# Rotary products on the tensor engine replaced by copies between partitions, in the sparse mixer of a two-block decoder

## The chip, the cores and the metric

One core of one Trainium2 chip. The metric is the device time of one execution in microseconds (us), the median of several runs. The kernel before takes 2184.75 us (median of 3 runs, 2183.49 to 2184.96). All data are float32; the matrix products of the weights are made in three passes on values split into a high and a low part.

## The reference, cut to what matters

The program is two decoder blocks of two mixers each on 512 tokens of width 1024. The change lies in the last mixer, the sparse attention ("NSA"), between its input projection and its scores:

```python
def rope(x, positions):                       # dh = 64
    inv = ROPE_THETA ** (-jnp.arange(0, dh, 2) / dh)
    ang = positions[..., None] * inv
    x1, x2 = jnp.split(x, 2, axis=-1)
    return jnp.concatenate([x1 * cos - x2 * sin, x2 * cos + x1 * sin], axis=-1)

p = h @ w_in                                  # 512 x 3632
q, kc, vc, ks, vs, kw, vw, gl, z = jnp.split(p, splits, axis=-1)
q = rope(q.reshape(B, S, 16, 64)) * 64 ** -0.5
kc, ks, kw = rope(...), rope(...), rope(...)  # 4 groups of 64 each
kcmp = compress(kc, pe_k, ck_w1, ck_w2)       # windows of 32 keys, stride 16, a small MLP
vcmp = compress(vc, pe_v, cv_w1, cv_w2)
# three softmax attentions of q: over kcmp/vcmp, over ks/vs, over kw/vw; gated and summed,
# times silu(z), and the product with w_out
```

## The kernel before, in words

Every engine has one program in a fixed order, written out by hand; engines meet through semaphores. The tensor engine runs the products; the scalar engine (ACT) makes the high part of each weight part ("WH", line 508), the vector engine (DVE) the low part ("WL", `dve_weights`, line 511), from "RAW", which the SP queue loads 1 MB (two parts) at a time into two buffers (`sync_weights`, line 495). WH and WL have three buffers, so the high part of part j waits until part j-3 has been used.

A feature (`feat`, line 585) is 24 products of 128x128 by 128x512 (8 pieces of the contraction, three passes each) into one PSUM bank: 128 rows of the projection (two heads or two groups of 64), 512 tokens wide. In the sparse mixer the tensor engine's program `pe_nsa` (line 2412) makes the gate logits and q features 0 and 1 together, turns the gate logits, makes q features 2 to 7, then the pairs kc0, kc1, vc0, vc1, ks0, ks1, the token products of the values (line 2460), `compress(0)`, kw0, kw1, more token products, `compress(1)`, and then the scores. "kc0" is the feature with groups 0 and 1 of the compressed keys.

The rotation (rope) swaps the two halves of each head, with a sign, and mixes them with cosines and sines. Before, the tensor engine makes the swap as a product with a permutation matrix that holds the sign:

- `rotate_q(m)` in `pe_nsa` (line 2421): one product of 128x128 by 128x512 on the copy of feature m that ACT has put into the temporary TM (line 2589). It stands one feature late: after feature m+1.
- `rotate_k(kind, pair)` (line 2426): for each of the two groups of the pair, one product that spreads the group over both halves of the partitions ("rda"), and one that spreads its swapped form ("rdb"); so four products for kc, ks and kw, and two for vc, which isn't rotated.
- DVE's `rotate_q` (line 2705) multiplies the product with the sines, TM with the cosines, and adds: three operations of 128x512. DVE's `rotate_k` (line 2713) does the same on each group, six operations a pair (eight for kc, whose second half is stored one token late, in "X2").
- ACT's `rotate_k` (line 2592) copies the spread vc from PSUM to X2.
- DVE's `gather` (line 2735) reads X2 for `compress`; the scores read KS and KW.

TM has four buffers in a ring. `turns()` (line 287) lists who takes them in turn and what must be done before the buffer is free: entry i waits for the end of entry i-4. Before, a q feature takes one entry, and the buffer of feature m is used again by feature m+4.

GpSimd (POOL) loads the mixer's constants and small weights, among them the first-layer weights of `compress(0)` (2 MB, "w1"), then waits for the end of `compress(0)` to load those of `compress(1)` into the same place (line 2912), and works again only in the scores (`share`).

Of the kernel before, what the change touches and what calls it, by code (L numbers as in the profile page):

```python
# [25 lines left out]
L_M, L_R, L_N = 0, 128, 640  # L26
N_NM, N_P, N_DA, N_DB, N_N = 0, 512, 640, 896, 1152
N_CM, N_CN, N_BD, N_IR, N_INV, N_N2 = 0, 128, 256, 260, 264, 266


def constants():
# [27 lines left out]

    def rot(src):  # L60

        m = np.zeros((128, 128), np.float32)
        for d in range(128):
            base, e = src[d]
            if e < 32:
                m[base + e + 32, d] = -1
            else:
                m[base + e - 32, d] = 1
        return m

    n[:, N_P:N_P + 128] = rot([(64 * (d // 64), d % 64) for d in range(128)])
    for par in range(2):
        a = np.zeros((128, 128), np.float32)
        for d in range(128):
            a[64 * par + d % 64, d] = 1
        n[:, N_DA + 128 * par:N_DA + 128 * par + 128] = a
        n[:, N_DB + 128 * par:N_DB + 128 * par + 128] = rot([(64 * par, d % 64) for d in range(128)])
    for t in range(4):
# [7 lines left out]
    inv = np.float32(10000.0) ** (-np.arange(0, 64, 2, dtype=np.float32) / np.float32(64))  # L86
    n2[:, N_INV] = inv.astype(np.float32)[p % 32]
    return {"c_base": c, "c_gdn": g, "c_alibi": b, "c_gla": l, "c_nsa": n, "c_nsb": n2}
# [98 lines left out]
class Book:  # L187
# [25 lines left out]
    def at(self, *event):  # L213
        if not self.known:
            return None, 0
        name, n = self.value[event]
        return self.sem(name), n
# [69 lines left out]
def turns():  # L287

    out = []
# [47 lines left out]
    out.append((("few", "n"), ("full", "few_t", "n")))  # L337
    out.extend((("rq", m), ("q", m)) for m in range(8))

    def rotated(kind, pair):  # L340
        if kind != "vc":
            for g in (2 * pair, 2 * pair + 1):
                out.extend((("rj", kind, g, i), ("kv", kind, g)) for i in range(2))

    before = None
    for kind, pair in (("kc", 0), ("kc", 1), ("vc", 0), ("vc", 1), ("ks", 0), ("ks", 1), ("kw", 0), ("kw", 1)):
        if before:
            rotated(*before)
        out.append((("rk", kind, pair), ("full", "rda" if kind == "vc" else "rdb", kind, pair, 1)))
        before = kind, pair  # L350
    rotated(*before)
    out.extend((("r4", g), ("full", "vcb")) for g in range(4))
# [5 lines left out]
def bass_decoder_pair(nc, I, K, out):  # L358
    with ExitStack() as ctx:
# [1980 lines left out]
        NM = CS[:, N_NM:N_NM + 512]  # L2340
        PRM = CS[:, N_P:N_P + 128]
        PE_R = slot(11)[0:32, 0:128]
# [41 lines left out]
        def value_gather(x, g):  # L2384

            x.wait_ge(*ps.free("rda", "vc", g // 2, g % 2))

# [24 lines left out]
        def pe_nsa(p):  # L2412
# [7 lines left out]

            def rotate_q(m):
                p.wait_ge(*ps.free("nq", m))
                p.wait_ge(*at("c_nsa"))
                several(p, ("nr", m), lambda b: [(b[:, :], PRM, tm("rq", m))])

            def rotate_k(kind, pair):
                p.wait_ge(*ps.free("nk", kind, pair))
                for par in range(2):
                    for name, col0 in (("rda", N_DA), ("rdb", N_DB)):
                        if name == "rda" or kind != "vc":  # L2430
                            several(p, (name, kind, pair, par), lambda b: [
                                (b[:, :], CS[:, col0 + 128 * par:col0 + 128 * par + 128], tm("rk", kind, pair))])

            def compress(i):
# [9 lines left out]
            for m in range(8):  # L2444
                if m >= 2:
                    feat(p, ("nq", m), NSA)
                if m:
                    rotate_q(m - 1)
            before = None
            for i, kind in enumerate(n_steps):  # L2450
                if kind:
                    feat(p, ("nk", *kind), NSA)
                if before:
                    rotate_k(*before)
                elif i == 0:
                    rotate_q(7)
                before = kind
                if not kind:
                    br = i // 7
                    toks(p, ("nvv", br), normed(NSA), 2, "V")  # L2460
                    if br:
                        p.wait_ge(*ps.free("cmp", 0, 1))
                        p.wait_ge(*at("w2_twice"))
                        job = ("keys",)
                        b = ps.take(*job)
                        p.wait_ge(*ps.empty(*job))
                        chain(p, PS[b][:, 0:128], [(W2D[:, m, :, :].rearrange("p e d -> p (e d)"), HD[:, 0, m, :])
                                                   for m in range(2)]).then_inc(*ps.filled(*job))
                    compress(br)
# [11 lines left out]
            def scores(u):  # L2481
# [8 lines left out]
                if br is None:  # L2490
# [8 lines left out]
                    return  # L2499
                p.wait_ge(*at("kv", "kw" if br else "ks", 3))  # L2500
                p.wait_ge(*at("mask"))
# [80 lines left out]
        def act_nsa(a):  # L2582
# [8 lines left out]

            def rotate_k(kind, pair):
                if kind == "vc":
                    for par in range(2):
                        g = 2 * pair + par
                        ba = bank("rda", kind, pair, par)
                        a.wait_ge(*ps.full("rda", kind, pair, par))
                        a.do.copy(X2[1][0:64, g, :], ba[0:64, :])
                        a.do.copy(X2[1][64:128, g, 0:511], ba[64:128, 1:512]).then_inc(*ps.read("rda", kind, pair, par))

            def compress(i):
                for m in range(2):
                    a.wait_ge(*ps.full("cmp", i, m))
                    act(a, HD[:, i, m, :], bank("cmp", i, m)[:, 0:128], ACT.Silu).then_inc(*ps.read("cmp", i, m))

            before = None
            for i, kind in enumerate(n_steps):
                if before:
                    rotate_k(*before)
                if kind:  # L2610
# [4 lines left out]
                else:  # L2615
# [7 lines left out]
                    compress(br)  # L2623
                before = kind

# [66 lines left out]
        def dve_nsa(v):  # L2692
# [12 lines left out]
            def rotate_q(m):  # L2705
                x, q = tm("rq", m), NQ[:, m, :]
                v.wait_ge(*ps.full("nr", m))
                v.wait_ge(*at("sines"))
                tt(v, q, bank("nr", m)[:, :], SIN, ALU.mult).then_inc(*ps.read("nr", m))
                step(v, tt(v, x, x, COS, ALU.mult))  # L2710
                tt(v, q, q, x, ALU.add).then_inc(*up("q", "q", m))

            def rotate_k(kind, pair):
                for par in range(2):
                    if kind == "vc":
                        continue
                    g = 2 * pair + par
                    job = (kind, pair, par)
                    t1, t2 = tm("rj", kind, g, 0), tm("rj", kind, g, 1)
                    v.wait_ge(*ps.full("rda", *job))  # L2720
                    v.wait_ge(*tm_clear("rj", kind, g, 0))
                    tt(v, t1, bank("rda", *job)[:, :], COS, ALU.mult).then_inc(*ps.read("rda", *job))
                    v.wait_ge(*ps.full("rdb", *job))
                    v.wait_ge(*tm_clear("rj", kind, g, 1))
                    tt(v, t2, bank("rdb", *job)[:, :], SIN, ALU.mult).then_inc(*ps.read("rdb", *job))
                    v.wait_ge(*ps.free("rda", *job))
                    v.wait_ge(*ps.free("rdb", *job))
                    if kind == "kc":
                        tt(v, X2[0][0:64, g, :], t1[0:64, :], t2[0:64, :], ALU.add)
                        m = tt(v, X2[0][64:128, g, 0:511], t1[64:128, 1:512], t2[64:128, 1:512], ALU.add)  # L2730
                    else:
                        m = tt(v, (KS if kind == "ks" else KW)[:, g, :], t1, t2, ALU.add)
                    m.then_inc(*up("kv", "kv", kind, g))

            def gather(i, piece):
# [6 lines left out]
                for g in (0, 1) if piece == 1 else (2, 3):  # L2742
                    if i:
                        value_gather(v, g)
                    else:
                        v.wait_ge(*at("kv", "kc", g))
                    base = X2[i][:, g, :]
# [145 lines left out]
        def pool_nsa(g):  # L2893
# [17 lines left out]
            load(g, "w1", ("w1", 0), W1, I["nsa_ck_w1_2"][0].rearrange("(l p) n -> p l n", p=128))  # L2911
            g.wait_ge(*ps.full("cmp", 0, 1))
            load(g, "w1", ("w1", 1), W1, I["nsa_cv_w1_2"][0].rearrange("(l p) n -> p l n", p=128))
            for i in range(-1, NT):
# [158 lines left out]
```

## Time and profile before

| | |
|---|---|
| median of 3 runs | 2184.75 us |
| the profiled execution's own time | 2184.13 us |
| its span in the profile | 2182.3 us |
| tensor engine (PE) busy | 2044.2 us, 94% of the span |
| VectorE (DVE) busy | 1081.5 us, 50% |
| ScalarE (ACT) busy | 901.0 us, 41% |
| GpSimd (POOL) busy | 178.3 us, 8% |
| mean granted clock of the tensor engine | 0.976 of full speed |

Times in the rows are microseconds from the span's start. The sparse mixer's projection runs from about 1735 to 1912, its scores and output product from there to the end. A row of the timeline tells start, length, engine, line, operation, what it writes and reads, and in brackets how long its engine had been idle and who released it. Matrix products overlap: the distance between two starts, not the length, tells what one costs. A float32 product of this kind leaves two records.

### The profile page before, as it was taken

To read this page: it belongs to the slowest core of one execution; us is meant where nothing else is said; L and a number is where in the kernel's file an instruction comes from. 1 tells how busy PE (TensorE), PEld (TensorE's weight loads), DVE (VectorE), ACT (ScalarE), POOL (GpSimd) and SP (SyncE) were. 2 spreads that over 40 slices of the span, in tenths; PEclk is the share of its full clock that TensorE was granted. 3 is DMA by queue.
4 is the path that set the end of the run, shared out by engine and by line. 5 is a ranking of instruction groups with operands and counts; after the bars stand their busy time and mean duration, and the time that the engine had idled before them with its cause. 6 is when DMAs were issued, how large, how long until landed. Compare 5 with 4: busy or idle time off the path is not lost. (4 is left out here: it accounts for less than half of the span.)

```text
span 2182.3 us, 27453 instructions
## 1 busy us (share of the span) xinstructions
PE 2044.2 (94%) x11261; PEld 1630.5 (75%) x11261; DVE 1081.5 (50%) x1728; ACT 901.0 (41%) x1661; POOL 178.3 (8%) x138
## 2 busy tenths in 40 slices
PE   7969989999999989999999999989999799989988
PEld 5758868888887777657888888767887677856567
DVE  4556545434435442674544343545255545455763
ACT  5552234323324553674432231464343522245562
POOL 1011000000000000440000000000000100033440
PEclk9989999999999999999999999998999899999999
DMA  4211112332322223111323332213321322210001
GB/s 140 74 58 40 40 58 87 97 97 97 97 97 78 77 86 97 39 39 58 107 97 96 97 97 97 78 53 98 97 68 39 96 95 75 80 39 20 20 2 68
DMA packets 117682, 162.41 MB, mean 74 GB/s; under 512 B 6074, under 2 KB 80070, under 8 KB 117558
## 3 DMA queue, kind: packets, MB, share of 16 engines
q1 hardware_dynamic: 114502, 150.47, 21.3%
q0 software_dynamic: 2768, 9.14, 1.4%
q8 instruction: 90, 1.47, 0.3%
q10 hardware_dynamic: 288, 1.05, 0.1%
q14 instruction: 34, 0.28, 0.0%
HBM read 158.55 MB, written 2.10 MB: 74 GB/s over the span
## 5 line engine op out<-in xcount | busy, mean ns | idle before, releaser
L438 DVE TENSOR_TENSOR WL<-RAW,WH 128x1024 fp32r<-128x1024 f32 (+1 forms) x283 | 346.0, 1225 | 410.4 <-ACT WH L508 409.9
L508 ACT CAST WH<-RAW 128x1024 fp32r<-128x1024 f32 (+1 forms) x283 | 292.8, 1037 | 401.1 <-PE PSUM L542 399.6
L542 PE MATMUL PSUM<-XH,WH 128*128 128x512 f32 (+4 forms) x1128 | 428.2, 380 | 7.0 <-DVE XL L438 3.6
L542 PE MATMUL PSUM<-XH,WL 128*128 128x512 f32 (+4 forms) x1128 | 415.2, 368 | 0.0
L542 PE MATMUL PSUM<-XL,WH 128*128 128x512 f32 (+4 forms) x1128 | 415.1, 368 | 0.0
L542 PE MATMUL PSUM<-WH,HP 128*128 128x512 f32 x1024 | 318.0, 390 | 1.9 <-DVE WL L438 1.9
L542 PE MATMUL PSUM<-WH,XH 128*128 128x512 f32 (+1 forms) x608 | 242.2, 398 | 20.2 <-DVE WL L438 13.4
L542 PEld LDWEIGHTS PSUM<-XH,WH 128*128 128x128 f32 (+3 forms) x1128 | 213.7, 189 | 48.6 <-issue 7.4
L542 PEld LDWEIGHTS PSUM<-XL,WH 128*128 128x128 f32 (+3 forms) x1128 | 213.2, 189 | 40.1 <-issue 6.3
L542 PEld LDWEIGHTS PSUM<-XH,WL 128*128 128x128 f32 (+3 forms) x1128 | 212.8, 189 | 35.5
L542 PE MATMUL PSUM<-WL,XH 128*128 128x512 f32 (+1 forms) x608 | 233.7, 384 | 0.0
L542 PE MATMUL PSUM<-WH,XL 128*128 128x512 f32 (+1 forms) x608 | 233.5, 384 | 0.0
L542 PEld LDWEIGHTS PSUM<-WH,HP 128*128 128x128 f32 x1024 | 192.3, 188 | 42.4 <-DVE WL L438 2.8
L455 ACT ACTIVATE TM<-PSUM 128x512 f32<-128x512 f32 x128 | 75.9, 597 | 317.8 <-PE PSUM L542 291.3
L542 PE MATMUL PSUM<-WL,HP 128*128 128x512 f32 x512 | 199.2, 389 | 0.0
L542 PEld LDWEIGHTS PSUM<-WH,XH 128*128 128x128 f32 x608 | 116.7, 192 | 49.7 <-DVE WL L438 16.6
L542 PEld LDWEIGHTS PSUM<-WL,XH 128*128 128x128 f32 x608 | 116.9, 192 | 22.9 <-issue 2.6
L542 PEld LDWEIGHTS PSUM<-WH,XL 128*128 128x128 f32 x608 | 116.5, 192 | 22.6
L438 DVE TENSOR_TENSOR TM<-TM 128x512 f32<-128x512 f32 x64 | 44.3, 692 | 173.9 <-ACT TM L455 173.4
L542 PEld LDWEIGHTS PSUM<-WL,HP 128*128 128x128 f32 x512 | 96.1, 188 | 19.9
L550 PE MATMUL PSUM<-AR 64*64 64x64 f32 (+6 forms) x1424 | 99.4, 262 | 10.2 <-ACT TM L455 6.7
L550 PEld LDWEIGHTS PSUM<-AR 64*64 64x64 f32 (+3 forms) x1424 | 75.9, 151 | 32.0 <-issue 20.0
(237 smaller groups left out, 2526.2 us busy)
## 6 DMA issues: line engine op xcount, KB each, us to landing
RAW<-in_w_mlp_dram SPq DMA_DIRECT2D x64, 1024.0 KB, 5.3
RAW<-in_nsa_w_in_dram SPq DMA_DIRECT2D x14, 1024.0 KB, 5.0
RAW<-in_w_in_e_dram SPq DMA_DIRECT2D x12, 1024.0 KB, 5.2
RAW<-in_w_qkv_o_dram SPq DMA_DIRECT2D x12, 1024.0 KB, 5.1
RAW<-in_gla_w_in_dram SPq DMA_DIRECT2D x12, 1024.0 KB, 5.2
RAW<-in_w_ple_gate_dram SPq DMA_DIRECT2D x8, 1024.0 KB, 5.0
RAW<-in_w_out_e_dram SPq DMA_DIRECT2D x4, 1024.0 KB, 4.9
RAW<-in_w_out_o_dram SPq DMA_DIRECT2D x4, 1024.0 KB, 5.1
```

The source lines that it names most:

```text
L438: return x.do.tensor_tensor(o, a, b, op)
L455: return a.do.activation(o, i, func, **kw)
L508: a.do.copy(hi, r).then_inc(*up("w_hi", "w_hi", j))
L542: m = p.do.matmul(o, l, r, start=start and i == 0, stop=stop and i == len(pairs) - 1)
L550: m = p.do.matmul(o, l, r, start=True, stop=True)
```

## The change

For q, kc, ks and kw the halves of each head are swapped by four DMAs of 32 partitions each, from one TM buffer ("rq" or "rk") to another ("rb"), issued by POOL (`swap_halves`). The sign stands in the frequencies of the constant, so the sines have it. DVE then rotates a whole pair of groups at once, in TM, with three operations of 128x512. For the keys four more DMAs of 64 partitions each spread the two groups over both halves of the partitions, straight into KS, KW or X2 (`spread`), one token late for the second half of X2. The permutation products, their constants (640 of the 1152 columns of c_nsa) and ACT's copies of vc are gone. The swap of q feature m takes two entries of the ring of TM. The first-layer weights of `compress(1)` are loaded from ACT's queue, since POOL is busy with other things there.

```diff
-    n[:, N_P:N_P + 128] = rot([(64 * (d // 64), d % 64) for d in range(128)])
...
-    n2[:, N_INV] = inv.astype(np.float32)[p % 32]
+    n2[:, N_INV] = np.where(p % 64 < 32, -1, 1) * inv.astype(np.float32)[p % 32]
...
-    out.extend((("rq", m), ("q", m)) for m in range(8))
...
+    for m in range(8):
+        out.extend(((("rq", m), ("q", m)), (("rb", m), ("q", m))))
+    for kind, pair in (("kc", 0), ("kc", 1), ("vc", 0), ("vc", 1), ("ks", 0), ("ks", 1), ("kw", 0), ("kw", 1)):
+        out.append((("rk", kind, pair), ("moved", kind, pair)))
         if kind != "vc":
+            out.append((("rb", kind, pair), ("rope", kind, pair)))
...
         def value_gather(x, g):
-            x.wait_ge(*ps.free("rda", "vc", g // 2, g % 2))
+            x.wait_ge(*at("moved", "vc", g // 2))
...
             for m in range(8):
                 if m >= 2:
                     feat(p, ("nq", m), NSA)
-                if m:
-                    rotate_q(m - 1)
-            before = None
             for i, kind in enumerate(n_steps):
                 if kind:
                     feat(p, ("nk", *kind), NSA)
-                if before:
-                    rotate_k(*before)
-                elif i == 0:
-                    rotate_q(7)
...
-                p.wait_ge(*at("kv", "kw" if br else "ks", 3))
+                for pair in range(2):
+                    p.wait_ge(*at("moved", "kw" if br else "ks", pair))
...
             def compress(i):          # ACT
...
+                if i == 0:
+                    load(a, "w1_values", ("w1", 1), W1, I["nsa_cv_w1_2"][0].rearrange("(l p) n -> p l n", p=128))
...
             def rotate_q(m):          # DVE
-                x, q = tm("rq", m), NQ[:, m, :]
-                v.wait_ge(*ps.full("nr", m))
+                x, y, q = tm("rq", m), tm("rb", m), NQ[:, m, :]
+                v.wait_ge(*at("rb", m))
                 v.wait_ge(*at("sines"))
-                tt(v, q, bank("nr", m)[:, :], SIN, ALU.mult).then_inc(*ps.read("nr", m))
+                tt(v, q, y, SIN, ALU.mult)
                 step(v, tt(v, x, x, COS, ALU.mult))
                 tt(v, q, q, x, ALU.add).then_inc(*up("q", "q", m))
 
             def rotate_k(kind, pair):
...
+                if kind == "vc":
+                    return
+                x, y = tm("rk", kind, pair), tm("rb", kind, pair)
+                v.wait_ge(*at("rb", kind, pair))
+                tt(v, y, y, SIN, ALU.mult)
+                step(v, tt(v, x, x, COS, ALU.mult))
+                tt(v, x, x, y, ALU.add).then_inc(*up("rope", "rope", kind, pair))
...
-            g.wait_ge(*ps.full("cmp", 0, 1))
-            load(g, "w1", ("w1", 1), W1, I["nsa_cv_w1_2"][0].rearrange("(l p) n -> p l n", p=128))
+            def swap_halves(*job):
+                x, y = tm("rq" if len(job) == 1 else "rk", *job), tm("rb", *job)
+                g.wait_ge(*ps.free(*(("nq",) if len(job) == 1 else ("nk",)), *job))
+                g.wait_ge(*tm_clear("rb", *job))
+                sem = f"swapped{tm_at['rb', *job] % 4}"
+                for d in range(4):
+                    s = d + 1 - 2 * (d % 2)
+                    load(g, sem, ("rb", *job) if d == 3 else (), y[32 * d:32 * d + 32, :], x[32 * s:32 * s + 32, :])
+
+            def spread(kind, pair):
+                x = tm("rk", kind, pair)
+                g.wait_ge(*(ps.free("nk", kind, pair) if kind == "vc" else at("rope", kind, pair)))
+                sem = f"spread{tm_at['rk', kind, pair] % 4}"
+                for par in range(2):
+                    src = x[64 * par:64 * par + 64, :]
+                    for r in range(2):
+                        last = ("moved", kind, pair) if par and r else ()
+                        if kind in ("ks", "kw"):
+                            load(g, sem, last, (KS if kind == "ks" else KW)[64 * r:64 * r + 64, 2 * pair + par, :], src)
+                        else:
+                            load(g, sem, last, X2[kind == "vc"][64 * r:64 * r + 64, 2 * pair + par, 0:512 - r], src[:, r:512])
+
+            for m in range(8):
+                swap_halves(m)
+            before = None
+            for kind in n_steps:
+                if kind and kind[0] != "vc":
+                    swap_halves(*kind)
+                if before:
+                    spread(*before)
+                before = kind
```

## Rows read from the trace of the kernel before

**Rows 1.** The page's first part: engines' busy time, share, instructions.

```profile
PE 2044.2 (94%) x11261; PEld 1630.5 (75%) x11261; DVE 1081.5 (50%) x1728; ACT 901.0 (41%) x1661; POOL 178.3 (8%) x138
```

**Rows 2.** Busy time in stretches of the mixer: PE, PEld, DVE, ACT, POOL, clock, DMA share.

```profile
1784.00:1803.00 19.00, 19.00 (x79) 14.63 (x78) 9.35 (x12) 4.60 (x6) 0.00 (x0) 1.00 0.22 70
1803.00:1835.00 32.00, 32.00 (x121) 22.41 (x120) 20.21 (x27) 10.78 (x16) 0.00 (x0) 1.00 0.17 58
```

**Rows 3.** Groups of PE instructions by shape, 1747 to 1912.

```profile
L550 PE MATMUL PSUM<-TM,CS 128*128 128x512 f32 x72 | 33.8, 596 | 4.1 <-ACT TM L455 3.0 <-ACT TM L2613 1.1
```

**Rows 4.** Timeline of PE: permutation products of q and of keys, and a feature.

```profile
1783.97 1.02 PE L550 MATMUL PSUM<-TM,CS 128*128 128x512 f32 x2
...
1787.37 0.39 PE L542 MATMUL PSUM<-XH,WL 128*128 128x512 f32 x1
...
1790.09 0.39 PE L542 MATMUL PSUM<-XH,WL 128*128 128x512 f32 x1
1790.32 1.02 PE L550 MATMUL PSUM<-TM,CS 128*128 128x512 f32 x2
...
1803.01 3.59 PE L550 MATMUL PSUM<-TM,CS 128*128 128x512 f32 x8
...
1820.79 1.88 PE L550 MATMUL PSUM<-TM,CS 128*128 128x512 f32 x4
...
1827.99 1.88 PE L550 MATMUL PSUM<-TM,CS 128*128 128x512 f32 x4
```

**Rows 5.** Timeline of PE where q feature 0 is swapped, and the next product.

```profile
1747.25 0.24 PE L557 MATMUL PSUM<-CB,AR 32*128 32x32 f32 x1
1750.54 1.13 PE L550 MATMUL PSUM<-TM,CS 128*128 128x512 f32 x2 [3.04 <-ACT TM L455]
...
1758.59 1.02 PE L550 MATMUL PSUM<-TM,CS 128*128 128x512 f32 x2
```

**Rows 6.** Busy time and granted clock just behind that wait.

```profile
1751.10:1755.10 4.00, 4.00 (x11) 2.99 (x10) 1.98 (x3) 0.00 (x0) 0.00 (x0) 0.58 0.18 60
```

**Rows 7.** Timeline of PE: the products of ks1 and kw1.

```profile
1839.33 3.70 PE L550 MATMUL PSUM<-TM,CS 128*128 128x512 f32 x8 [0.53 <-ACT TM L2613]
...
1876.58 3.70 PE L550 MATMUL PSUM<-TM,CS 128*128 128x512 f32 x8 [0.54 <-ACT TM L2613]
```

**Rows 8.** Timeline of ACT: the copies of q features 0 and 1, and a later step.

```profile
1749.91 1.07 ACT L455 ACTIVATE TM<-PSUM 128x512 f32<-128x512 f32 x2
...
1790.52 0.60 ACT L455 ACTIVATE TM<-PSUM 128x512 f32<-128x512 f32 x1 [4.81 <-PE PSUM L542]
```

**Rows 9.** Timeline of DVE: the rotation of one q feature and a low part.

```profile
1785.03 0.69 DVE L438 TENSOR_TENSOR AR<-PSUM,AR 128x512 f32<-128x512 f32 x1 [3.20 <-PE PSUM L550]
...
1786.96 1.22 DVE L438 TENSOR_TENSOR WL<-RAW,WH 128x1024 fp32r<-128x1024 f32 x1
```

**Rows 10.** Timeline of POOL: an issue and its next work; DVE beside the issue.

```profile
1734.02 1.22 DVE L438 TENSOR_TENSOR WL<-RAW,WH 128x1024 fp32r<-128x1024 f32 x1
...
1734.94 0.50 POOL L463 DMA_DIRECT2D AR<-in_nsa_pe_k_dram  x1
...
1861.99 1.15 POOL L463 DMA_DIRECT2D AR<-in_nsa_cv_w_dram  x1 [122.89 <-PE PSUM L542]
1920.63 0.61 POOL L438 TENSOR_TENSOR AR<-AR,ST 128x256 f32<-128x256 f32 x1 [57.49 <-DVE ST L438]
```

**Rows 11.** DMA issues by tensor: KB each, us from issue to landing.

```profile
AR<-in_gla_w_gk_up_dram POOLq DMA_DIRECT2D x1, 32.0 KB, 3.3
out_dram<-H SPq DMA_DIRECT2D x4, 512.0 KB, 2.6
AR<-in_nsa_pe_v_dram POOLq DMA_DIRECT2D x1, 8.0 KB, 4.8
AR<-in_nsa_b_gate_dram POOLq DMA_DIRECT2D x1, 24.0 KB, 7.7
AR<-in_nsa_cv_w_dram POOLq DMA_DIRECT2D x1, 2048.0 KB, 10.2
```

More of the change, by code:

```diff
@@ L26 @@
 L_M, L_R, L_N = 0, 128, 640
-N_NM, N_P, N_DA, N_DB, N_N = 0, 512, 640, 896, 1152
+N_NM, N_N = 0, 512
 N_CM, N_CN, N_BD, N_IR, N_INV, N_N2 = 0, 128, 256, 260, 264, 266
@@ L58, in constants @@
     n[:, N_NM:N_NM + 512] = np.where(x <= j, 0, NEG)
[L60 to L69, printed above, removed]
-    n[:, N_P:N_P + 128] = rot([(64 * (d // 64), d % 64) for d in range(128)])
[L72 to L77, printed above, removed]
     for t in range(4):
@@ L337, in turns @@
     out.append((("few", "n"), ("full", "few_t", "n")))
-    out.extend((("rq", m), ("q", m)) for m in range(8))
-    def rotated(kind, pair):
+    for m in range(8):
+        out.extend(((("rq", m), ("q", m)), (("rb", m), ("q", m))))
+    for kind, pair in (("kc", 0), ("kc", 1), ("vc", 0), ("vc", 1), ("ks", 0), ("ks", 1), ("kw", 0), ("kw", 1)):
+        out.append((("rk", kind, pair), ("moved", kind, pair)))
         if kind != "vc":
-            for g in (2 * pair, 2 * pair + 1):
-                out.extend((("rj", kind, g, i), ("kv", kind, g)) for i in range(2))
-    before = None
-    for kind, pair in (("kc", 0), ("kc", 1), ("vc", 0), ("vc", 1), ("ks", 0), ("ks", 1), ("kw", 0), ("kw", 1)):
-        if before:
[L348 to L351, printed above, removed]
+            out.append((("rb", kind, pair), ("rope", kind, pair)))
     out.extend((("r4", g), ("full", "vcb")) for g in range(4))
@@ L2340, in bass_decoder_pair @@
         NM = CS[:, N_NM:N_NM + 512]
-        PRM = CS[:, N_P:N_P + 128]
         PE_R = slot(11)[0:32, 0:128]
@@ L2419, in pe_nsa @@
             turned(p, ("pec",), lambda b: [(b[:, 0:32], PE_R)])
[L2421 to L2432, printed above, removed]
             def compress(i):
@@ L2446, in pe_nsa @@
                     feat(p, ("nq", m), NSA)
-                if m:
-                    rotate_q(m - 1)
-            before = None
             for i, kind in enumerate(n_steps):
@@ L2452, in pe_nsa @@
                     feat(p, ("nk", *kind), NSA)
-                if before:
-                    rotate_k(*before)
-                elif i == 0:
-                    rotate_q(7)
-                before = kind
-                if not kind:
+                else:
                     br = i // 7
@@ L2590, in act_nsa @@
                 act_weights(a, first_part["nq", m] + 3)
[L2592 to L2599, printed above, removed]
             def compress(i):
@@ L2604, in compress @@
                     act(a, HD[:, i, m, :], bank("cmp", i, m)[:, 0:128], ACT.Silu).then_inc(*ps.read("cmp", i, m))
-            before = None
+                if i == 0:
+                    load(a, "w1_values", ("w1", 1), W1, I["nsa_cv_w1_2"][0].rearrange("(l p) n -> p l n", p=128))
             for i, kind in enumerate(n_steps):
-                if before:
-                    rotate_k(*before)
                 if kind:
@@ L2623, in act_nsa @@
                     compress(br)
-                before = kind
             def z_gate(m):
@@ L2713, in rotate_k @@
             def rotate_k(kind, pair):
[L2714 to L2733, printed above, removed]
+                if kind == "vc":
[5 more added lines that the diff above has]
+                tt(v, x, x, y, ALU.add).then_inc(*up("rope", "rope", kind, pair))
             def gather(i, piece):
@@ L2745, in gather @@
                     else:
-                        v.wait_ge(*at("kv", "kc", g))
+                        v.wait_ge(*at("moved", "kc", g // 2))
                     base = X2[i][:, g, :]
@@ L2911, in pool_nsa @@
             load(g, "w1", ("w1", 0), W1, I["nsa_ck_w1_2"][0].rearrange("(l p) n -> p l n", p=128))
-            g.wait_ge(*ps.full("cmp", 0, 1))
-            load(g, "w1", ("w1", 1), W1, I["nsa_cv_w1_2"][0].rearrange("(l p) n -> p l n", p=128))
+            def swap_halves(*job):
[16 more added lines that the diff above has]
+                            load(g, sem, last, (KS if kind == "ks" else KW)[64 * r:64 * r + 64, 2 * pair + par, :], src)
+                        else:
+                            load(g, sem, last, X2[kind == "vc"][64 * r:64 * r + 64, 2 * pair + par, 0:512 - r], src[:, r:512])
[8 more added lines that the diff above has]
+                before = kind
             for i in range(-1, NT):
```

## The prediction, made before the change was timed

> **What bounds the kernel now.** I read the page first [rows 1]: the tensor engine is busy for 94% of the span, the vector engine for 50%, POOL for 8%. An average says nothing of one stage, so the table by stretches comes next [rows 2]: from 1784 to 1835 PE is busy for all of the time, DVE for 9.35 of 19.00 us and 20.21 of 32.00 us, at a full clock, while the DMA engines are busy for 0.22 and 0.17. In this stage a microsecond taken off PE should be a microsecond of the kernel, as long as nothing new is late. What the change takes off PE is one group [rows 3]: 72 records, 36 products (8 for q, 24 for kc, ks, kw, 4 for vc), 33.8 us busy and 4.1 us of idle time ahead of them, which waited for ACT's copies.
>
> **What goes from PE.** Busy times overlap, so I price a product by starts [rows 4].
> - A feature: from 1787.37 to 1790.09 there are 12 starts, 0.2267 us each; 24 make 5.44 us.
> - A q step is 1790.32 - 1783.97 = 6.35, so a q product costs 6.35 - 5.44 = 0.91; eight: 7.3 us.
> - A rotated pair: from kc0's products to vc0's, two steps, 1820.79 - 1803.01 = 17.78, so 8.89 a step; less 5.44 is 3.45; six pairs: 20.7 us.
> - vc: 1827.99 - 1820.79 = 7.20, less 5.44 is 1.76; two: 3.5 us. Together 31.5 us.
> - The wait of q product 0 for ACT's copy, 3.04 us [rows 5]. After the change nothing on PE waits for that copy; the next feature's parts are made by then.
> - The clock behind that wait. From product 0 to product 1 it is 1758.59 - 1750.54 = 8.05 us against 6.35 in the later step: 1.70 us. The row of that stretch shows a granted clock of 0.58, near the lower level of 1.2 GHz, where the later stretches have 1.00 (2.4 GHz) [rows 6, 2]. PE had been idle just before. Without the idle time I expect no fall: 1.7 us more.
> - The waits ahead of the products of ks1 and kw1, 0.53 + 0.54 = 1.1 us [rows 7].
> Sum: 31.5 + 3.0 + 1.7 + 1.1 = 37.3 us.
>
> **What comes in its place, q.** Say feature m ends at t. ACT's copy starts about 0.2 later and takes 0.5 to the next start (two take 1.07 [rows 8]). POOL issues four DMAs; an issue takes 0.50 [rows 10], so the fourth starts 1.5 after the first. No row shows a copy from SBUF to SBUF. Bounds for the landing from its issue: 2.6 us for a store of 512 KB (SBUF is its source), 7.7 us for 24 KB that queued behind other loads; the nearest row by size and queue is 32 KB on POOL's queue, 3.3 us [rows 11]. I take 3.3. Then DVE needs three operations, from 1785.03 to 1786.96, 1.93 us [rows 9], the same number as before. End: t + 0.2 + 0.5 + 0.1 + 1.5 + 3.3 + 1.9 = t + 7.5. Two deadlines follow.
> - The ring of TM. The copy of feature m+2 now needs q(m), since a feature takes two entries; it comes up at t + 10.9. Slack 3.4 us.
> - DVE's order. Behind the blocked rotation of m stands the low part that is used four features on, which starts at t + 16.3; it is done at t + 7.5 + 1.2 [rows 9]. Slack over 7 us in the steady run, but less at the start, as copies 0 and 1 are late (1749.91 and about 1750.4 [rows 8]): swap 0 can't start before 1750.6, q(0) is done at 1757.2, then copy 2, its high part, the rotation of 1 and the low part of feature 5 at 1760.4. PE, running from 1747.4 at 5.44 a step, wants that part at 1763.8: slack 3.4 us, the tightest place.
>
> **The keys.** Let kc0 end at T. POOL has kc1's swap ahead of kc0's spread, so: swap of kc1 from T + 6.3 to T + 8.3, four issues of the spread to T + 10.3, the last one's landing 3.3 after its start at T + 9.8: T + 13.1. ACT's copy of vc0 waits for that buffer, 2 us beyond vc0's end, and with it the high part behind it on ACT (T + 14.6) and the low part on DVE (T + 15.8). ks1 uses it at T + 21.8: slack 6 us. I carried all programs through such a schedule, step by step, to the scores: with 3.3 us PE never waits. It stays so up to a landing of 4.5 us; 5.0 costs 0.4, 6.7 costs 8.5 and 7.7 costs 14.5 us. Run on the program before, the same schedule gives its end within 1 us, once the 1.7 of the clock are added.
>
> **Edits at no cost, with their cover.** DVE's six or eight operations a pair become three: less on an engine that waits [rows 2]. ACT's eight copies of vc go. The smaller constant lands sooner; nobody waits for it. POOL's 88 new issues, 44 us at 0.50 [rows 10], lie in its empty stretch: one issue stands between about 1739 and 1920. Loading w1 for compress(1) from ACT: issued at the end of compress(0), as before, it lands 10.2 us later [rows 11]; two features (10.9) and the value products stand between: over 10 us of slack. ACT's issue delays kw0's copy, which has that feature's 5.4 us as cover. If this cover goes, compress(1) waits. The scores' new wait for ks stands 45 us behind the spread. The transfers, 3.6 MB of swaps and 4 MB of spreads, meet SP's loads, 1 MB every two steps; the DMA share is about 0.2 there [rows 2]. A swap that meets such a load may take 5 to 6 us; in the schedule that is every other one, and those may be 6 us late in landing before PE stands.
>
> **A rule weighed against a row.** An issue at 1734.94 takes 0.50 us although DVE is at a subtraction with two operands from SBUF until 1735.24 [rows 10]. The Trainium skill (SBUF — State Buffer, "The 'DVE blocks DMA' trap (SWDGE)") says that a DVE operation in a two-port mode, as a float32 copy has, locks POOL out, so that it cannot write descriptors. DVE has no such copy beside the swaps, only two memsets; with each issue at the 0.50 of the row the sum stands, and with the issues of one swap held back by up to the 3.4 us of slack above it would stand too.
>
> **The numbers.** The profiled execution has 2184.13 us, its span 2182.3, and the median is 2184.75, 0.6 above. 2184.13 - 37.3 = 2146.8; on the median 2147.5. That is the forecast, and alone it would lie between 2146 and 2149.
>
> **Rivals.**
> - **Late landings, some given back.** The four transfers of a swap meet SP's loads or each other, and the last lands after 6 to 9 us. For: 7.7 us for only 24 KB in a full queue [rows 11]. Against: there the queue had 1 MB loads and more ahead of it. The schedule gives back 5 to 24 us: 2152 to 2171, about 2159 at 7 to 7.5 us. Chance 0.18.
> - **The transfers run one after another (slower).** If POOL's transfers don't overlap but each pays its whole latency, the queue, not PE, sets the pace. From q 0 to ks1 there are 72 (48 of swaps, 24 of spreads) against about 72 us of features: PE waits from 1.3 us each, and from 1.75 us each all 37 us are gone. At the lower landing of 2.6 us [rows 11] each, the schedule loses 113 - 37 = 76 us: about 2260. Against: 8 KB that were the third of a row of loads issued about 0.5 us apart on this queue landed after 4.8 us [rows 11], less than three latencies of 2.6. Chance 0.07. The Trainium skill (DMA: Bandwidth & Descriptors, "Rules for kernel authors") says that two transfers to disjoint halves of the partitions serialize, and gives a fixed cost of about 2.0 us for each; by that, at 2.15 us each, the schedule would lose 73 - 37 = 36 us: 2221.
> - **The time saved isn't there.** The weight parts, not PE, would set the pace once a step is 5.44 instead of 6.35 us. Against: from 1784 to 1803, three steps, DVE is busy for 9.35 and ACT for 4.60 us [rows 2], 3.1 and 1.5 a step. Then no difference, 2184. Chance 0.02.
> - **The gain is cut in the scores:** PE comes 37 us earlier, but spreads or w1 don't. A wait of 10 us for w1 behind transfers of spreads: 2158. Chance 0.05.
>
> **How the numbers follow.** Forecast 0.68, late landings 0.18, scores 0.05, no difference 0.02, slower 0.07. The range 2145.5 to 2166 holds the forecast, the scores and most of the late landings (up to about 8 us); it leaves out the far end of that, and the two others, some 0.15 in all. Its lower end is the forecast less 2 us for a product priced too low. 0.2% is 4.4 us, about what a measurement of this kernel can tell from no change. Faster: 0.68 + 0.18 + 0.05 = 0.91; same 0.02; slower 0.07.
>
> **What would show it.** In the profile after, the group of 72 records is gone, starts of features stand 5.44 us apart without a wait of PE from 1747 on, the clock stays at 1.00 behind 1747, POOL has about 44 us more of issues, the swaps' landing is near 3.3 us and the scores begin some 37 us earlier. Waits of PE for DVE's low parts, ahead of q features 5 and 6 or ks1, would show late landings; landings that grow from one transfer to the next would show that they serialize.

## The result, and the profile after

| | before | after |
|---|---|---|
| median | 2184.71 us (4 runs) | 2152.45 us (4 runs, 2148.84 to 2153.83) |
| ratio, 95% interval | | 0.9851 [0.9834, 0.9868] |
| the profiled execution's own time | 2184.13 us | 2151.18 us |
| its span | 2182.3 us | 2149.4 us |

The ratio is the time after divided by the time before. The kernel is 32.3 us faster; 37.3 were forecast. The first part of the page after, which answers to [rows 1]:

```profile
PE 2014.3 (94%) x11189; PEld 1618.7 (75%) x11189; DVE 1066.8 (50%) x1706; ACT 896.9 (42%) x1653; POOL 221.3 (10%) x225
```

The 72 records of the permutation products are gone (11261 to 11189), and POOL has 43 us more of work, its DMA issues. Busy time by stretch (columns as in [rows 2]) shows PE without a gap and at full clock from 1748.5 to 1865, where before it lost time at 1750 [rows 5, 6]:

```profile
1748.50:1760.00 11.50, 11.50 (x51) 9.52 (x52) 6.16 (x10) 5.09 (x8) 5.63 (x12) 1.00 0.51 145
1760.00:1800.00 40.00, 40.00 (x178) 33.12 (x177) 24.46 (x32) 10.99 (x15) 17.07 (x35) 1.00 0.59 169
1800.00:1865.00 65.00, 65.00 (x446) 60.24 (x445) 32.45 (x47) 18.10 (x29) 21.23 (x43) 1.00 0.70 187
```

POOL's timeline: two swaps, then one, and so on, each four issues in 1.96 us, 0.49 an issue. From the fourth on, swaps of q start 5.44 us apart (1760.66, 1766.10, 1771.54), which is the pace of PE's features, so they follow PE and do not lead it:

```profile
1751.90 3.99 POOL L437 DMA_DIRECT2D TM<-TM  x8 [11.68 <-ACT TM L429]
1758.36 1.96 POOL L437 DMA_DIRECT2D TM<-TM  x4 [2.46 <-ACT TM L429]
1760.66 1.97 POOL L437 DMA_DIRECT2D TM<-TM  x4 [0.34 <-ACT TM L429]
1766.10 1.96 POOL L437 DMA_DIRECT2D TM<-TM  x4 [3.48 <-ACT TM L429]
1771.54 1.96 POOL L437 DMA_DIRECT2D TM<-TM  x4 [3.48 <-ACT TM L429]
```

The DMA issues by tensor (KB each, median us to landing; answers to [rows 11]):

```profile
TM<-TM POOLq DMA_DIRECT2D x56, 64.0 KB, 2.0
AR<-TM POOLq DMA_DIRECT2D x24, 128.0 KB, 2.7
AR<-in_nsa_cv_w_dram ACTq DMA_DIRECT2D x1, 2048.0 KB, 8.3
AR<-TM POOLq DMA_DIRECT2D x8, 127.8 KB, 3.2
```

A swap's transfer lands 2.0 us from its issue in the median, faster than the lower bound of 2.6 that I had from a store. The median hides that some came late. The same view of two stretches, 1758.4 to 1760.2 and 1760.7 to 1762.6, each with the issues of one swap of q:

```profile
TM<-TM POOLq DMA_DIRECT2D x4, 64.0 KB, 1.9
...
TM<-TM POOLq DMA_DIRECT2D x4, 64.0 KB, 5.0
```

They are the swaps issued from 1758.36 and 1760.66. Beside the second stands a load of SP: 1 MB, issued between 1759 and 1761, landed after 6.0 us. One more swap of the fourteen, at 1771.54, landed after 3.4 us, and single transfers of spreads after up to 7.3. PE waited for none of them: from 1740 to 1868 its list of waits is empty. So where did 5 us go? To find it, I cut each trace at three landmarks, events that exist in all of them: POOL's issue of the load of c_nsa (1734.40 before, 1735.53 after), PE's product of the compressed values ("XN,TM", 1904.71 and 1868.16), and POOL's first share of 128x1024 (1922.03 and 1891.32).

| stretch, us | before | after | difference |
|---|---|---|---|
| to the load of c_nsa | 1734.40 | 1735.53 | +1.1 |
| c_nsa to compressed values: the projection | 170.31 | 132.63 | -37.7 |
| compressed values to first large share | 17.32 | 23.16 | +5.8 |
| from there to the end | 260.27 | 258.08 | -2.2 |

The projection gives what the prediction's sum said. The loss is in the next stretch. PE's timeline there, after:

```profile
1868.16 1.89 PE L516 MATMUL PSUM<-XN,TM 128*128 128x64 f32 x16
1872.63 1.92 PE L2447 MATMUL PSUM<-XN,AR 64*128 64x32 f32 x16 [2.58 <-DVE AR L412]
...
1882.02 0.39 PE L516 MATMUL PSUM<-XH,WL 128*128 128x512 f32 x1
1885.28 1.40 PE L2458 MATMUL PSUM<-AR 64*128 64x512 f32 x4 [2.87 <-issue]
```

and before:

```profile
1904.71 1.89 PE L542 MATMUL PSUM<-XN,TM 128*128 128x64 f32 x16
1906.54 1.08 PE L2495 MATMUL PSUM<-XN,AR 64*128 64x32 f32 x16
...
1912.89 0.39 PE L542 MATMUL PSUM<-XH,WL 128*128 128x512 f32 x1
1913.21 1.13 PE L2505 MATMUL PSUM<-AR 64*128 64x512 f32 x4
```

Between the values' product and the second scores there were 8.5 us and are now 17.1. Two waits are new: 2.58 us for DVE ahead of the first scores, 2.87 ahead of the second, which the view puts down to "issue". DVE's timeline names it: both end when DVE has read a z feature out of its PSUM bank (0.69 us from 1871.68 and from 1884.49).

```profile
1871.68 0.69 DVE L412 TENSOR_TENSOR AR<-PSUM,AR 128x512 f32<-128x512 f32 x1 [7.61 <-ACT AR L429]
...
1884.49 0.69 DVE L412 TENSOR_TENSOR AR<-PSUM,AR 128x512 f32<-128x512 f32 x1 [7.67 <-ACT AR L429]
```

Behind the first wait the granted clock is at 0.50 (1.2 GHz) for 6.4 us, while PE makes the first scores and the first part of z feature 1. From the start of these scores to the last product of z feature 1 it takes 1882.02 - 1872.63 = 9.4 us, where it took 1912.89 - 1906.54 = 6.35 before:

```profile
1868.00:1872.60 4.60, 2.05 (x18) 1.87 (x16) 0.69 (x1) 4.17 (x5) 0.00 (x0) 0.97 0.00 0
1872.60:1879.00 6.40, 6.37 (x27) 5.37 (x28) 4.06 (x11) 0.42 (x1) 0.00 (x0) 0.50 0.51 164
1879.00:1882.40 3.40, 3.40 (x15) 2.49 (x13) 0.00 (x0) 0.00 (x0) 0.00 (x0) 0.97 0.00 0
```

Why do the scores wait for a z feature? `Banks.take` (line 236 before) hands out the eight PSUM banks in turn, and the scores have fixed ones (0 and 1, then 2 and 3). The permutation products took 36 banks: 8 for q, 24 for the rotated keys, 4 for vc. 36 is 4 more than a multiple of 8, so without them every later bank in turn is moved by four. Counted through the program: z feature 0, the compressed values and z feature 1 were in banks 5, 6, 7; now they are in 1, 2, 3. The first scores must wait for z feature 0 to be read from bank 1, the second for z feature 1 in bank 3.

### The profile page after: what moved, and what is told of

It reads as the page before. It is cut to its first block and busy times, and to the rows that moved or that the text cites. A ratio compares the mean times of both kernels' runs of the same rounds, so it can differ in the third digit from the quotient of the medians.

```text
span 2149.4 us, 27350 instructions
## 1 busy us (share of the span) xinstructions
PE 2014.3 (94%) x11189; PEld 1618.7 (75%) x11189; DVE 1066.8 (50%) x1706; ACT 896.9 (42%) x1653; POOL 221.3 (10%) x225
## 5 line engine op out<-in xcount | busy, mean ns | idle before, releaser
L516 PE MATMUL PSUM<-XH,WH 128*128 128x512 f32 (+4 forms) x1128 | 423.0, 375 | 7.8 <-DVE XL L412 4.4
```

The lines of the kernel that those rows point to most:

```text
L516: m = p.do.matmul(o, l, r, start=start and i == 0, stop=stop and i == len(pairs) - 1)
```

## The experiments

**1. The old banks under the changed kernel.**

```diff
+            ps.next = (ps.next + 4) % 8
             feat(p, ("nz", 0), NSA)
```

> The changed kernel, with the PSUM bank that is next in turn moved on by four ahead of z feature 0, so that z feature 0, the compressed values and z feature 1 get banks 5, 6 and 7 again, as in the kernel before, in place of 1, 2 and 3. Theory (the missing gain is a collision of banks): the two waits of PE of 2.6 and 2.9 us ahead of the first scores go, and the fall of the clock behind the first; the projection then gains all of the 37.3 us of the prediction, and the time is 2145 to 2149 us, ratio to before 0.982 to 0.984. Rival (the missing 5 us are a cost of the DMAs, or lie elsewhere): no change, 2151 to 2153 us, ratio 0.985.

Measured: 2145.02 us (5 runs, 2143.16 to 2146.88), ratio 0.9822 [0.9808, 0.9835] to 2183.6 us before. One line gives back what was missing, and this kernel beats both. It is 7.4 us faster than the changed kernel by the medians. The stretch explains 5.8 of that; in the two traces 2.9 us more lie ahead of the projection (the load of c_nsa at 1732.61 against 1735.53), where both kernels are the same. The projection takes 132.66 us, the stretch behind it 17.32 us, as before the change. PE's only wait from 1740 to 1884:

```profile
PE PSUM L2475 <- POOL AR L412: 5.5, 1, 5.5
```

It is the wait for POOL's first share, the small one of 128x256 just ahead of the large one, which the kernel before has too (5.46 us, until 1921.30).

**2. The new banks under the kernel before**, the same line and nothing of the swaps:

> The kernel before, with the same move of four banks: z feature 0, the compressed values and z feature 1 get banks 1, 2 and 3; nothing of the swaps is touched. Bank theory: waits of PE of some 2.6 and 2.9 us appear ahead of the first scores, and the kernel is slower by 3.5 to 7.5 us, 2188 to 2192 us. Rival (the DMAs cost it): no change, 2184.7 us.

Measured: 2188.21 us (11 runs, 2186.71 to 2191.69), ratio 1.0019 [1.001, 1.0027]: 4.6 us slower, at the near end of what was expected. The projection is unchanged (170.29), the next stretch has 23.04 us (17.32 before), the rest 258.13 (260.27 before), and the two waits appear, from 1900 to 1925:

```profile
PE PSUM L2506 <- issue: 2.9, 1, 2.9
PE PSUM L2496 <- DVE AR L438: 2.5, 1, 2.5
```

The loss needs no DMA. With experiment 1 this settles the cause of the 5.8 us in the stretch: the collision alone makes them, and its absence alone takes them away.

**3. Another placing**, `ps.next + 2`: banks 3, 4, 5.

> The changed kernel with the next bank moved on by two: banks 3, 4 and 5. The first scores use banks 0 and 1, the second ones 2 and 3. Bank theory: no wait ahead of the first scores; z feature 0 in bank 3 is read before the second ones; z features 2 to 7, all in bank 7, need not wait for z feature 1. Equal to the run with 5, 6 and 7 within 1 us, or up to 2 us faster: 2143 to 2149 us. Rival (only the old placing is good, the collision moves elsewhere): 2150 us or more.

Measured: 2146.03 us (4 runs, 2144.73 to 2146.7), ratio 0.9824 [0.981, 0.9837]; stretches 132.64 and 17.32 us. Not the old numbers matter, only that the fixed ones are kept clear. There is no further gain from z features 2 to 7, which here need not wait for feature 1: PE's waits in them behind the share are 6.7 us in this run and in experiment 1 alike.

**4. What each collision costs.** The line stands behind the compressed values, so only z feature 0 collides:

```diff
             step_(-2)
+            ps.next = (ps.next + 4) % 8
             feat(p, ("nz", 1), NSA)
```

> The changed kernel, with the next bank moved on by four only behind z feature 0 and the compressed values: z feature 0 in bank 1, the compressed values in 2, z feature 1 in 7. It tells what each of the two collisions costs. Theory: the first scores wait 2.6 us for the reading of z feature 0, and z feature 1 behind them runs at the lower clock for about 4 us (some 2.3 us more); the second wait goes. From the compressed values' product to the first large share on POOL 20 to 22 us, where it is 17.3 without and 23.2 with both collisions; the time lies 1 to 4 us above the run without. If the second collision alone makes the loss, it is as without, 17.3 us.

Measured: 2147.98 us (4 runs), ratio 0.9835 [0.982, 0.9849]; the stretch takes 22.58 us, a little above what was expected. The wait of 2.6 us is there, the second is gone, and PE waits 5.1 us for POOL's share instead (1.2 with both collisions). So in this stretch the first collision costs nearly all, 5.3 of 5.8 us: 2.6 of waiting, and the rest with the clock behind it, again 0.50 for 6.4 us. The second mostly replaces a wait that would come anyway. The whole times do not show this split: this kernel is 3.0 us above experiment 1 and 4.5 below the changed kernel. What the stretch leaves over lies, in the traces, ahead of the projection (c_nsa at 1732.61 in experiment 1, 1733.15 here, 1735.53 in the changed kernel) and behind the share (258.81, 256.61 and 258.08 us), where nothing was changed.

**5. q alone by DMA**, keys and vc by products (24 + 4 banks as before, so 8 fewer and no shift):

> Only the q features are swapped by DMA, the keys and vc stay with the products (their matrices without the sign, since the sines have it). Eight banks less are taken, so the banks of z stay 5, 6 and 7. By the prediction's sum: 7.3 (eight products) + 3.0 (the wait) + 1.7 (the clock) = 12.0 us less, 2172.7 us, ratio 0.9945. Rival (the swaps are not hidden behind the features): less than 9 us gained, 2176 us or more.

Measured: 2167.78 us (4 runs), ratio 0.9928 [0.9914, 0.9941], 15.8 us less. The projection takes 158.41 us, 11.9 less than before, where the sum said 12.0. The remaining 3.9 lie outside the change, 3.6 of them in the trace behind the share: see the last section.

**6. The keys alone by DMA**, q by products, old banks of z:

> Only kc, ks, kw and vc are swapped and spread by DMA, q keeps its eight products (matrix without the sign); banks of z 5, 6 and 7. By the prediction's sum: 20.7 + 3.5 (products) + 1.1 (two waits) = 25.3 us less than before, ratio 0.9885; from the start of the constant's load to the compressed values' product 25.3 us less in the trace. With the 11.9 us that q alone took off the same stretch that makes the whole of 37.6. Rival (the spreads of the keys cost part of it): under 22 us.

Measured: 2154.96 us (4 runs), ratio 0.9865 [0.9851, 0.988], 30.5 us less, where the sum said 25.3. The projection takes 144.53 us (1736.03 to 1880.56), 25.8 less; 25.3 were expected. 11.9 + 25.8 = 37.7, which is what the projection of the changed kernel gained. Here too the surplus lies outside it (256.82 us behind the share, 260.27 before). The 3.0 us of [rows 5] are still there, as they belong to q:

```profile
PE PSUM L525 <- ACT TM L430: 3.0, 1, 3.0
```

**7 and 8. How much slack the swaps have.** On the kernel of experiment 1, each swap in eight transfers (two halves of the columns), and in twelve:

```diff
-                for d in range(4):
+                cuts = (0, 176, 352, 512)   # or (0, 256, 512)
+                for c0, c1 in zip(cuts, cuts[1:]):
+                    for d in range(4):
...
+                        load(g, sem, ("rb", *job) if d == 3 and c1 == 512 else (), y[32 * d:32 * d + 32, c0:c1], x[32 * s:32 * s + 32, c0:c1])
```

> The changed kernel with banks 5, 6 and 7, and each swap issued as eight transfers of 32 partitions by 256 columns in place of four by 512: 2.0 us more of POOL's issues a swap, 28 us in all. Theory (swaps lie beside the features as long as they keep the slack of 3.4 us of the prediction's schedule): slower than the run with banks as before by 0 to 1.5 us, 38 to 36.5 us faster than before. Rival (the swap stands in the path of PE): slower by most of 14 x 2.0 = 28 us.

> As the last, with twelve transfers a swap (176, 176 and 160 columns): 4.0 us more a swap than with four, beyond the slack. Theory: PE waits about 3.3 to 4.8 us for the low part of q feature 5, then about 0.4 us in most steps and 2 us at ks1, since POOL needs 5.9 us a swap and a feature lasts 5.44; together 8 to 10 us slower than with four transfers. Rival (slack is far larger than the schedule says): no loss. Rival (each microsecond counts): 14 x 4.0 = 56 us slower.

Eight: 2146.17 us (4 runs), ratio 0.9831 [0.9815, 0.9848]. 28 us more of issues cost 0.6 us of projection (133.28), 1.2 by the medians, and one wait of PE, ahead of a product of the compression:

```profile
PE PSUM L516 <- DVE AR L412: 0.4, 1, 0.4
```

Twelve: 2162.15 us (4 runs), ratio 0.9897 [0.9882, 0.9911]. Past the slack the cover is gone. POOL issues 48 transfers on end, and PE waits for DVE's low parts, which stand behind the blocked rotations (timelines of POOL and PE):

```profile
1754.29 23.56 POOL L437 DMA_DIRECT2D TM<-TM  x48 [11.68 <-ACT TM L429]
```

```profile
1770.51 0.50 PE L516 MATMUL PSUM<-XH,WH 128*128 128x512 f32 x1 [2.92 <-DVE WL L412]
...
1779.38 0.79 PE L516 MATMUL PSUM<-XH,WH 128*128 128x512 f32 x1 [3.13 <-DVE WL L412]
```

The projection loses 147.38 - 132.66 = 14.7 us, where the schedule said 8 to 10. The waits of PE in it sum to 10.1 us for low parts and 1.4 us ahead of the compression; the rest is partly the clock behind the longer ones (0.91 from 1770 to 1790). By the medians it is 17.1 us above experiment 1; 5.3 us of that lie, in the traces, ahead of the projection (c_nsa at 1737.91 against 1732.61). "No slack" (56 us) and "much more slack" (no loss) both fall.

## Why the prediction was right, and which term was missing

The direction and the range (2145.5 to 2166) held; the forecast of 2147.5 was 5 us too low, beyond its own narrow range of 2146 to 2149. The wide range had been opened for late landings, which cost nothing here, and for a loss in the scores of another cause. That it also took in the loss that came is luck. By its steps:

- **The products, the first wait, the clock behind it, the two waits at ks1 and kw1: 37.3 us.** Right: the projection is 37.7 us shorter, and q and keys separately 11.9 and 25.8 against 12.0 and 25.3. Products priced by the distance of starts, 31.5 us, made this exact; with the group's busy time [rows 3], 33.8 us, in their place the sum would have been 39.6.
- **The swap's duration.** Issue 0.49 us, 0.50 taken from [rows 10]; landing 2.0 us in the median where 3.3 was taken, for the spreads 2.7 to 3.2 us. The term was too high, on the harmless side. Bounds from loads out of the main memory said little of a copy within SBUF.
- **A swap that meets a load of SP** was to take 5 to 6 us, and every other one was to meet one. One of fourteen took 5.0 and one 3.4 us, and PE waited for neither. So the late landings of the first rival exist, but stayed within the slack.
- **The slack of 3.4 us** at the low part of q feature 5. With the landing 1.3 us faster it should be 4.7. Two swaps stand ahead of it, so experiments 7 and 8 lengthen the way to it by 4 and 8 us: no wait, and 3.3 us. Measured: none there, and 2.92 us. The place and the size were right. The steps beyond were not: in place of 0.4 us in most of them, PE waited 3.13 us for the next feature's part and 1.42, 1.22 and 1.47 us for three later ones, and the loss was put too low.
- **vc0's copy waits for kc0's spread.** As foretold: ACT waited 5.6 us for a DMA there, and PE didn't.
- **POOL's 44 us of issues at no cost.** 43 us, and at no cost.
- **The Trainium skill's rule on POOL being locked out by DVE** (SBUF — State Buffer, "The 'DVE blocks DMA' trap (SWDGE)"): issues of 0.49 us in four beside DVE's work show no lock-out, as the row had said of operations with two SBUF operands. The prediction says that DVE has no float32 copy beside the swaps. It has two short ones, between swaps in the changed kernel, and in experiment 8 POOL issues beside them (timelines of POOL and DVE):

```profile
1857.69 2.94 POOL L437 DMA_DIRECT2D TM<-TM  x6
1858.84 0.23 DVE L2702 COPY XN<-XN 128x128 f32<-128x128 f32 x1
1858.98 0.23 DVE L2703 COPY XN<-XN 128x128 f32<-128x128 f32 x1
```

  Six issues in 2.94 us are again 0.49 each, so copies this short show no lock-out of the issues. Their transfers landed late, after some 5.3 us, but so did those issued just ahead of them (5.5 to 5.9) and behind (5.0), beside loads of SP. No run has a long copy there.
- **The Trainium skill's rule on serializing halves** (DMA: Bandwidth & Descriptors, "Rules for kernel authors"): four transfers issued within 2 us land 2.0 us (median of 56) from their own issues, so they do not wait for each other's whole latency here, and the slower rival fell by that. No run shows what the rule makes of large transfers.
- **The rival "the gain is cut in the scores"** had the right place and the wrong cause: neither spreads nor w1 were late. What failed is the part "edits at no cost, with their cover". It went through engines, queues and buffers of TM, and left out a resource that removed products release: 36 turns of the PSUM banks. The missing term is + 5.8 us in the stretch ahead of the first share. In the profiled executions 37.3 us were forecast and 32.9 came. Within 0.1 us this is 37.3 less 5.8 lost in the stretch and 1.1 ahead of the projection, plus 0.4 more gained in the projection and 2.2 behind the share. Just behind the share the clock stays at 1.00 with the collision, where it is 0.62 without it in the kernel before; PE had waited 1.2 us for POOL's share there, and 5.5 before:

```profile
1891.32:1896.32 5.00, 5.00 (x32) 3.59 (x31) 2.06 (x4) 3.30 (x10) 2.83 (x2) 1.00 0.01 3
```

  That may be part of the 2.2 us, and experiment 2 has the same 2.1; but this last part also varies between kernels without a collision (last section), so how much of it the collision gives back is not shown.

## What to carry to other kernels

When a change adds or takes away an allocation in a round-robin pool (banks, buffers, semaphores), count how far it moves all later ones, and look where fixed ones begin; a neutral-looking removal can lay a producer onto a buffer that is wanted at once. A short wait of PE costs more than itself if the clock falls behind it: 2.6 us of waiting made 5.3. A transfer hidden beside steady work is free up to its slack and then costs again and again (0.6 us with eight transfers, 14.7 with twelve), so work the slack out from the ring's length and the order on the blocked engine, and test it by lengthening the transfer.

## What was not expected of the hardware

The same work from the first large share to the end takes 260.27 us in the trace of the kernel before, 258.81 in experiment 1 and 256.65 in q alone, none of which has the collision. Rows by stretch at the same distances from that share, 0 to 5 us and 200 to 210 us behind it: before,

```profile
1922.03:1927.03 5.00, 5.00 (x19) 2.75 (x19) 0.44 (x1) 1.78 (x6) 1.90 (x1) 0.62 0.00 0
...
2122.03:2132.03 10.00, 7.51 (x23) 5.95 (x24) 0.80 (x3) 2.94 (x15) 4.22 (x3) 0.66 0.16 53
```

experiment 1,

```profile
1882.59:1887.59 5.00, 5.00 (x18) 2.66 (x18) 0.34 (x1) 1.71 (x5) 1.89 (x1) 0.60 0.00 0
...
2082.59:2092.59 10.00, 7.47 (x35) 6.34 (x36) 1.68 (x5) 3.57 (x17) 4.26 (x3) 0.83 0.17 54
```

and q alone:

```profile
1909.45:1914.45 5.00, 5.00 (x26) 3.36 (x26) 1.26 (x2) 2.30 (x6) 1.90 (x1) 0.80 0.00 0
...
2109.45:2119.45 10.00, 8.39 (x45) 7.17 (x46) 1.67 (x4) 2.65 (x12) 3.34 (x3) 1.00 0.15 52
```

PE's wait at each of these rows is the same in all three: 5.46 us for POOL's share just ahead of the first, and in the second this one (before, experiment 1, q alone):

```profile
2124.52 0.79 PE L542 MATMUL PSUM<-WH,XH 128*128 128x512 f32 x1 [2.81 <-ACT AR L455]
2085.12 0.80 PE L516 MATMUL PSUM<-WH,XH 128*128 128x512 f32 x1 [2.81 <-ACT AR L429]
2111.06 0.50 PE L543 MATMUL PSUM<-WH,XH 128*128 128x512 f32 x1 [2.81 <-ACT AR L456]
```

The mean granted clock of those ten microseconds is 0.66 in one, 0.83 in the next and 1.00 in the third. Ahead of the change the traces differ as well: POOL's load of c_nsa stands at 1732.61 in experiment 1 and at 1737.91 in experiment 8, with the same program up to there. A change can so be worth 2 to 4 us more or less than its own stage shows: q alone and keys alone gain 15.8 + 30.5 = 46.3 us by their medians, the whole (experiment 1) 38.6 us, but by the projection 11.9 + 25.8 = 37.7 and 37.7. Why the clock falls in one kernel and not in the other behind the same wait stays open; no run was made for it.
